# Joints between products in token halves, and retention in chunks of 128 tokens

## The chip, the cores and the metric

The kernel runs on one core of a Trainium2 chip. The metric is the device time of one execution in microseconds (us); before the change it was 2417.52, the median of three runs from 2414.93 to 2419.92. A core has TensorE (PE in the rows, its weight loads PEld), VectorE (DVE), ScalarE (ACT), GpSimd (POOL) and SyncE (SP), which issues the transfers here. Each engine works through its own instruction list in order and waits on semaphores for the others.

## The reference

Input `x` is 512 tokens by 1024 channels in float32. Two stacks of layers follow each other. The first has a mixer of four groups of heads (retention, gated delta, two gated linear ones), attention to a memory, and a feed-forward layer. The second has two layers, each with a mixer, a feed-forward part, norms before and after, and factors computed from a condition. What the change touches:

```python
def rms_norm(x, g):                                   # over the 1024 channels of a token
    y = x * lax.rsqrt(jnp.mean(x * x, axis=-1, keepdims=True) + EPS)
    return y * g

# second stack, layer i, twice (mixer, then feed-forward):
h = rms_norm(x, norm_pre) * (1.0 + sc) + sh
y = mixer(h)                                          # ends with @ w_out; the other ends with @ w_down
x = x + (1.0 + g) * rms_norm(y, norm_post)

# retention, one head, chunks of c tokens (the reference takes c = 64):
scores = (q @ k.T) * decay                            # decay = exp(lg * (i - j)) for i >= j, inside the chunk
o      = scores @ v + (q @ state) * exp(lg * (i + 1))
state  = state * exp(lg * c) + (k * exp(lg * (c - 1 - j))).T @ v
```

Every value of `c` gives the same `o`; one chunk of 512 needs no state.

## The kernel before

Activations lie with channels on the 128 partitions and tokens along a row: 1024 channels are 8 tiles (KT) of 128 x 512. A product's weights are streamed from memory by SyncE into a ring of six slots. A weight tile (up to 8 inner blocks of 128 x 128) is split by VectorE into a high and a low part (`split_until`, L344 and L346; ScalarE does some of the first), which needs one of three slots of `high`. Each inner step of an output tile is three matmuls in a rounded format, high x high, low x high and high x low (`passes`, L393 to L395), each on 512 token columns into one PSUM bank. `product` goes over the output tiles; with `lead=2` its first two output tiles advance together, inner step by inner step, as the input tiles become ready (`inputs_ready`).

**A joint** (`edge`, L451) is what lies between the last product of one part and the first of the next in the second stack: `ab_out` (16 inner steps) to `up_1`, `down_1` (22) to `sc_in`, `sc_out` (8) to `up_2`; and `down_2` (22) to the output. `plain_product` (L2671) computes the product before it: ScalarE takes each output tile out of PSUM twice, squared (L2699) and plain (L2701); GpSimd adds the squares (L419). Then, on 512 tokens at a time:

1. TensorE sums the squares over the channels, 128 equal columns per token block (L473, L476). ScalarE takes the root (L496), VectorE the reciprocal (L518), TensorE spreads it over the partitions (`spread_root`, L465).
2. Per tile j of 8: VectorE multiplies `y` by the factor and the gain (L530) and adds it to the residual `h` (L534); ScalarE squares the new `h` (L508); TensorE adds it up (L487).
3. Root, reciprocal and spread again. Per tile: VectorE scales `h` (L541), ScalarE adds the shift and rounds (L513), VectorE makes the low part (L547). The next product's led tiles take each tile as it comes.

`keep_busy` (L653, its matmul L656) issues n products of a constant that nobody reads: 11 ahead of step 2, one after each of its tiles, 8 after the second spread. In the last joint there is no step 3, and `store_output` (L3546) stores tile by tile behind L534.

**Retention** is a part of `mixers` (L1482), in the first stack. The order of TensorE's work there is written out by hand, one call after another (L1873 on). It is interleaved with a triangular inverse (`inverse_times`, L1679) in 32 x 32 pieces and followed by `join_first` (L1697), `join_second` (L1707, L1711). `ret_scores(i)` (L1650) computes for a pair of heads m and a key block j the scores of 128 keys with all later queries (512, 384, 256 or 128 columns), VectorE multiplies them by the decay (`ret_weight`, L2222, 16 operations of L2228), and `ret_values(i)` (L1663) adds the values product; eight such steps, through two pairs of score banks.

A float32 matmul (constants, sums, retention) stands in the trace as two pieces. The sections of the diff below name the functions again.

## Time and profile before

| what | value |
|---|---|
| median of three runs | 2417.52 us |
| the profiled execution's own time | 2420.88 us |
| its span, first to last instruction | 2419.1 us |
| mean granted TensorE clock | 0.973 |
| busy: PE, DVE, ACT, POOL | 2335.3, 1651.3, 663.9, 183.2 us |
| memory traffic | 253.94 MB, 105 GB/s |

The profile shows one execution. Busy time of an engine is the sum of its instructions' durations; matmuls overlap, so a busy PE can still be below its peak. "PEclk" is the clock that TensorE was granted as a share of full speed. A row in order of time has the start, the duration, engine, line, operation, output and inputs with their shape, the count of merged instructions, and in brackets how long the engine had been idle and who released it; "issue" means that nothing in the profile held it. Durations of neighbouring VectorE or ScalarE operations overlap a little, so the distance from start to start is the better price.

### The profile page before, as it was taken

Reading aid. Unit: us, or ns where it says so; the run is one execution under the profiler, and the core shown is the slowest. Engines: PE = TensorE matmul, PEld = TensorE weight load, DVE = VectorE, ACT = ScalarE, POOL = GpSimd, SP = SyncE. Lnnn points to the kernel's source line nnn. Section 1 sums busy time; section 2 is a strip of 40 time slices with the busy share of each in tenths; the row PEclk is TensorE's granted clock in tenths of the full one; section 3 lists DMA queues with packets and bytes.
Section 4 is the critical chain, followed back from the end, with each engine's and each line's share of the span. In section 5 each row is a group of like instructions: output and inputs, shape, how many; then the busy total and the mean of one; then the engine's idle time right before and its main releaser. Section 6 shows DMA issues by size and latency. Waiting matters only on the chain.

```text
span 2419.1 us, 35289 instructions
## 1 busy us (share of the span) xinstructions
PE 2335.3 (97%) x14624; PEld 1898.2 (78%) x14624; DVE 1651.3 (68%) x2569; ACT 663.9 (27%) x1200; POOL 183.2 (8%) x179
## 2 busy tenths in 40 slices
PE   8998879999999999999989999999999999999997
PEld 6886668878888888887756788888888888888886
DVE  6674366756888865559788777666667886666653
ACT  2321253022211201324768413222102113222200
POOL 0001222001000011003211010000010000000000
PEclk9999579999999999999999999999999999999998
DMA  4220003412222453322200361232562451322341
GB/s 183 79 79 2 21 3 122 158 52 88 96 96 96 135 204 130 107 81 92 88 1 2 138 219 62 98 100 97 197 214 104 182 186 63 102 96 96 127 141 64
DMA packets 71728, 253.94 MB, mean 105 GB/s; under 512 B 8560, under 2 KB 8848, under 8 KB 71056
## 3 DMA queue, kind: packets, MB, share of 16 engines
q1 hardware_dynamic: 71280, 251.14, 30.4%
q8 instruction: 116, 1.90, 0.3%
q10 hardware_dynamic: 288, 0.54, 0.1%
q14 instruction: 44, 0.36, 0.0%
HBM read 247.97 MB, written 2.10 MB: 103 GB/s over the span
## 4 chain that ended last, share of the span: by engine, by line
PE 47%; DVE 3%; issue 0%; ACT 0%; POOL 0%; DVEq 0%; POOLq 0%
PE psum L393 14%; PE psum L394 14%; PE psum L395 13%; PE psum L3362 1%; PE psum L487 1%; PE psum L3349 1%; PE psum L3384 1%; DVE scratch L3440 1%; DVE scratch L3416 1%; PE psum L656 0%; PE psum L3376 0%; PE psum L465 0%; DVE h L534 0%; DVE n L530 0%; PE psum L476 0%
## 5 line engine op out<-in xcount | busy, mean ns | idle before, releaser
L393 PE MATMUL psum<-rounded_n,rounded_high 128*128 128x512 f32 x1824 | 722.1, 396 | 8.0 <-DVE rounded_ring L346 4.6
L394 PE MATMUL psum<-rounded_n_low,rounded_high 128*128 128x512 f32 x1824 | 712.1, 390 | 0.0
L395 PE MATMUL psum<-rounded_n,rounded_ring 128*128 128x512 f32 x1824 | 712.0, 390 | 0.0
L346 DVE TENSOR_TENSOR rounded_ring<-ring,rounded_high 128x1024 fp32r<-128x1024 f32 (+1 forms) x360 | 448.4, 1246 | 43.5 <-ACT rounded_high L329 31.5
L393 PEld LDWEIGHTS psum<-rounded_n,rounded_high 128*128 128x128 f32 x1824 | 343.9, 189 | 86.6 <-issue 7.4
L394 PEld LDWEIGHTS psum<-rounded_n_low,rounded_high 128*128 128x128 f32 x1824 | 344.1, 189 | 74.2 <-issue 3.9
L395 PEld LDWEIGHTS psum<-rounded_n,rounded_ring 128*128 128x128 f32 x1824 | 343.7, 188 | 72.1
L344 DVE CAST rounded_high<-ring 128x1024 fp32r<-128x1024 f32 (+1 forms) x347 | 250.4, 722 | 188.3 <-PE psum L395 177.9
L393 PE MATMUL psum<-rounded_arena,rounded_high 128*128 128x512 f32 x720 | 280.2, 389 | 0.0
L395 PE MATMUL psum<-rounded_arena,rounded_ring 128*128 128x512 f32 x720 | 280.1, 389 | 0.0
L394 PE MATMUL psum<-rounded_arena,rounded_high 128*128 128x512 f32 x720 | 280.1, 389 | 0.0
L2617 DVE SCALAR_TENSOR_TENSOR scratch<-arena,vecs,scratch 128x512 f32<-128x512 f32 x88 | 65.9, 748 | 162.8 <-ACT scratch L2604 162.8
L393 PEld LDWEIGHTS psum<-rounded_arena,rounded_high 128*128 128x128 f32 x720 | 135.1, 188 | 28.3 <-issue 0.2
L395 PEld LDWEIGHTS psum<-rounded_arena,rounded_ring 128*128 128x128 f32 x720 | 135.1, 188 | 28.1
L394 PEld LDWEIGHTS psum<-rounded_arena,rounded_high 128*128 128x128 f32 x720 | 135.1, 188 | 27.9
L2598 ACT COPY arena<-psum 128x512 f32<-128x512 f32 x88 | 51.7, 587 | 351.2 <-PE psum L395 351.2
L2604 ACT ACTIVATE scratch<-arena,vecs 128x512 f32<-128x512 f32 x88 | 63.8, 725 | 188.4 <-DVE arena L2638 186.9
L2699 ACT ACTIVATE scratch<-psum 128x512 f32<-128x512 f32 x32 | 19.2, 600 | 317.4 <-PE psum L395 317.4
L419 POOL TENSOR_TENSOR sum_sq<-sum_sq,scratch 128x512 f32<-128x512 f32 x38 | 59.9, 1575 | 288.4 <-ACT scratch L2699 242.2
L416 POOL COPY sum_sq<-scratch 128x512 f32<-128x512 f32 x6 | 4.7, 786 | 955.4 <-ACT scratch L2699 820.0
L993 DVE CUSTOM_DVE_ANT_0 arena<-arena 128x1024 f32<-128x1024 f32 x48 | 61.9, 1333 | 13.4 <-DMA arena<-in_mod_w 13.4
L993 DVE CUSTOM_DVE_ANT_0 n_low<-n_low 128x1024 f32<-128x1024 f32 x48 | 56.7, 1221 | 19.9 <-DMA n_low<-in_mod_w 19.9
(507 smaller groups left out, 2798.3 us busy)
## 6 DMA issues: line engine op xcount, KB each, us to landing
ring<-in_w_up SPq DMA_DIRECT2D x132, 512.0 KB, 3.6
ring<-in_w_down SPq DMA_DIRECT2D x48, 512.0 KB, 3.5
n_low<-in_mod_w SPq DMA_DIRECT2D x48, 512.0 KB, 5.8
arena<-in_mod_w SPq DMA_DIRECT2D x48, 512.0 KB, 5.3
ring<-in_w_ab_in SPq DMA_DIRECT2D x37, 512.0 KB, 3.6
ring<-in_w_mix_in SPq DMA_DIRECT2D x31, 512.0 KB, 3.6
ring<-in_w_sc_in SPq DMA_DIRECT2D x24, 512.0 KB, 5.7
ring<-in_w_down SPq DMA_DIRECT2D x24, 384.0 KB, 3.0
```

Of the source, the lines that this page charges most:

```text
L344: nc.vector.tensor_copy(self.rounded(high), raw).then_inc(self.weights_rounded, 1)
L346: nc.vector.tensor_tensor(self.rounded(raw), raw, self.rounded(high), ALU.subtract).then_inc(self.weights_split, 1)
L393: self.nc.tensor.matmul(out, w_high, x_high, start=first, stop=False)
L394: self.nc.tensor.matmul(out, w_high, x_low, start=False, stop=False)
L395: return self.nc.tensor.matmul(out, w_low, x_high, start=False, stop=last)
L419: nc.gpsimd.tensor_tensor(total, total, sq, ALU.add).then_inc(added, 1)
L487: last = nc.tensor.matmul(k.psum[:, SUMS + c, P:2 * P], k.squares[:, j % 2, c * P:(c + 1) * P], ones, start=(j == 0), stop=(j == KT - 1))
L993: k.nc.vector.tensor_tensor_reduce(out=self.tiles[:, i % 3], in0=self.tiles[:, i % 3], in1=self.cond, scale=1.0, scalar=0.0, op0=ALU.mult, ...
L2598: nc.scalar.copy(x, k.psum[:, j % PRODUCT_BANKS, :]).then_inc(out, 1)
L2604: nc.scalar.activation(dst, x, ACT.Copy, scale=taps[:, col:col + 1]).then_inc(tapped, 1)
L2617: link(nc.vector.scalar_tensor_tensor(dst, src[:, 0:T], taps[:, col:col + 1], dst, ALU.mult, ALU.add))
L3349: last = nc.tensor.matmul(k.psum[:, 2 * (m % 2) + s, at * P:(at + nk) * P], k.z[rows, NQT + p, i * P:(i + 1) * P], k.z[rows, (KS, KW)[b] + ...
```

## The change

**Joints.** The last output tile of the product before a joint is computed as two halves of 256 tokens (`last_tile`), the second into another bank. The sums of half 0 are put between the matmuls of the second half (`meanwhile`): sums at inner step 2, the spread at 6, column sums of the new `h` at 13, 15, and so on. The sums have one column instead of 128. Updates, squares, scalings and low parts are done per half (h = 0, 1); five of eight residual additions per half go to GpSimd (`POOL_ADDS`). The next product's two led tiles run through all inner steps for half 0 and then for half 1 (`halves=2`), and half 1's updates, squares and column sums are placed beside half 0's steps (`beside`). How much of half 0 is placed ahead of the second half's eviction depends on the inner length: `early` is 8 for 22 steps, 4 for 16, 0 for 8; `late` (for 22) also shifts half 1 by two steps. The fillers are now 2, 2, 3 and 3 products. The output is stored in halves.

**Retention.** Scores are computed within chunks of 128 tokens only (16 products 128 x 128). The state at each chunk's start comes from `ret_grow` (12 products 64 x 64 of the keys, turned into token rows by 8 more transposes and weighted in `ret_tails`) and `ret_grown_states` (five short VectorE operations); `ret_values` adds state x query to scores x values. GpSimd scales the queries first (two operations). The 16 weightings are four of 512 columns.

On TensorE, at the joint after `ab_out`, a row of the program's order names the line, the operation, output and inputs, the columns and how often it is repeated. Before:

```order
L395 MATMUL psum<-rounded_arena,rounded_ring 128x512
L473 MATMUL psum<-consts,sum_sq 128x128 x4
L476 MATMUL psum<-consts,scratch 128x128 x4
L465 MATMUL psum<-consts,roots 128x128 x4
L656 MATMUL psum<-consts 128x128 x11
L487 MATMUL psum<-consts,scratch 128x128 x4
L656 MATMUL psum<-consts 128x128
```

At its end before:

```order
L487 MATMUL psum<-consts,scratch 128x128 x4
L465 MATMUL psum<-consts,roots 128x128 x4
L656 MATMUL psum<-consts 128x128 x8
L393 MATMUL psum<-rounded_n,rounded_high 128x512
L394 MATMUL psum<-rounded_n_low,rounded_high 128x512
L395 MATMUL psum<-rounded_n,rounded_ring 128x512
```

After, from the end of the last tile's second half (L421 to L423 are `passes`, L829 the filler, L542 a column sum of the new `h`, L526 and L527 the sums of half 1, L534 and L549 the two spreads):

```order
L423 MATMUL psum<-rounded_arena,rounded_ring 128x256
L542 MATMUL psum<-consts,scratch 128x1 x6
L526 MATMUL psum<-consts,sum_sq 128x1
L527 MATMUL psum<-consts,scratch 128x1
L526 MATMUL psum<-consts,sum_sq 128x1
L527 MATMUL psum<-consts,scratch 128x1
L829 MATMUL psum<-consts 128x128 x2
L542 MATMUL psum<-consts,scratch 128x1 x4
L829 MATMUL psum<-consts 128x128 x2
L542 MATMUL psum<-consts,scratch 128x1 x4
L534 MATMUL psum<-consts,roots 128x128 x2
L829 MATMUL psum<-consts 128x128 x3
```

The sums of half 0 have moved into the last tile, those of half 1 stand behind it, and the fillers are fewer and in other places.

On VectorE, the same joint before, from the last update of step 2 on (L530, L534) to the scalings and low parts of step 3 (L541, L547):

```order
L530 SCALAR_TENSOR_TENSOR n<-n,mod_cols,psum 128x512
L534 TENSOR_TENSOR h<-h,n 128x512
L518 RECIPROCAL roots<-roots 128x4
L541 SCALAR_TENSOR_TENSOR n_low<-h,mod_cols,psum 128x512 x2
L547 SCALAR_TENSOR_TENSOR rounded_n_low<-n_low,mod_cols,rounded_n 128x512
L541 SCALAR_TENSOR_TENSOR n_low<-h,mod_cols,psum 128x512
L547 SCALAR_TENSOR_TENSOR rounded_n_low<-n_low,mod_cols,rounded_n 128x512
```

After, from half 0's last update on; L664 and L668 are the update and the addition, L673 the scaling, L679 the low part, L349 and L351 the split of a weight tile:

```order
L668 TENSOR_TENSOR h<-h,n 128x256
L660 RECIPROCAL roots<-roots 128x2 x2
L349 CAST rounded_high<-ring 128x1024
L351 TENSOR_TENSOR rounded_ring<-ring,rounded_high 128x1024
L673 SCALAR_TENSOR_TENSOR n_low<-h,mod_cols,psum 128x256
L664 SCALAR_TENSOR_TENSOR n<-n,mod_cols,psum 128x256
L673 SCALAR_TENSOR_TENSOR n_low<-h,mod_cols,psum 128x256
L664 SCALAR_TENSOR_TENSOR n<-n,mod_cols,psum 128x256
L668 TENSOR_TENSOR h<-h,n 128x256
L679 SCALAR_TENSOR_TENSOR rounded_n_low<-n_low,mod_cols,rounded_n 128x256
```

A split and half 1's updates now stand between the scalings and the low parts of half 0.

On TensorE in the mixer, before, from the last steps of retention to the first joining product (L1660 scores, L1669 values, L1679 and L1697 the inverse):

```order
L1660 MATMUL psum<-z 128x384 x2
L1679 MATMUL psum<-ring 32x32 x64
L1669 MATMUL psum<-ring,n_low 64x512 x2
L1660 MATMUL psum<-z 128x256 x2
L1679 MATMUL psum<-high,ring 32x32 x64
L1669 MATMUL psum<-ring,n_low 64x384 x2
L1660 MATMUL psum<-z 128x128 x2
L1669 MATMUL psum<-ring,n_low 64x256 x2
L1697 MATMUL psum<-ring,n 32x32 x32
```

After (L1833 scores, L1868 and L1886 the inverse, L1780 transposes, L1843 the states' growth, L1859 values, L1855 state x query):

```order
L1780 MATMUL psum<-consts,z 128x128 x8
L1868 MATMUL psum<-ring 32x32 x64
L1833 MATMUL psum<-z 128x128 x8
L1868 MATMUL psum<-high,ring 32x32 x64
L1843 MATMUL psum<-n_low,n 64x64 x12
L1868 MATMUL psum<-ring 32x32 x64
L1868 MATMUL psum<-high,ring 32x32 x64
L1859 MATMUL psum<-ring,n_low 64x128 x2
L1855 MATMUL psum<-z,n 64x128 x2
```

The scores now stand in two groups ahead, and all the values products behind the inverse.

The diff, cut to its core:

```diff
+        for h in range(halves if lead > 1 else 0):
+            cols = tokens(h) if halves > 1 else slice(0, width)
+            for k in range(kt):
+                if inputs_ready is not None:
+                    pe.wait_ge(inputs_ready, kt * h + k + 1)
+                for j in range(lead):
+                    if h == 0 and k == 0:
+                        if banks_free is not None:
+                            pe.wait_ge(banks_free[0], banks_free[1] - PRODUCT_BANKS + j + 1)
+                        pe.wait_ge(self.weights_split, first + j + 1)
+                    x = [part[:, cols] for part in rhs(k)]
+                    last = self.passes(self.psum[:, j % PRODUCT_BANKS, cols], first + j, k, x, k == 0, k == kt - 1)
+                    if h == halves - 1 and k == kt - 1:
+                        last.then_inc(self.weights_used, 1)
+                if beside is not None:
+                    beside(kt * h + k)
...
+    def last_tile(self, pe, name, rhs, evacuated, first_half, meanwhile):
+
+        n_out, kt = PRODUCTS[name]
+        j, first = n_out - 1, self.first_tile[name] + (n_out - 1) * self.chunks(name)
+        for h in range(2):
+            pe.wait_ge(evacuated, j + h - PRODUCT_BANKS + 1)
+            out = self.psum[:, (j + h) % PRODUCT_BANKS, tokens(h)]
+            for kk in range(kt):
+                i = first + kk // SLOT_KT
+                if h == 0 and kk % SLOT_KT == 0:
+                    pe.wait_ge(self.weights_split, i + 1)
+                x = [part[:, tokens(h)] for part in rhs(kk)]
+                last = self.passes(out, i, kk % SLOT_KT, x, kk == 0, kk == kt - 1)
+                if h == 0 and kk == kt - 1:
+                    last.then_inc(first_half, 1)
+                if h == 1:
+                    if kk % SLOT_KT == SLOT_KT - 1 or kk == kt - 1:
+                        last.then_inc(self.weights_used, 1)
+                    meanwhile(kk)
...
+    kt = PRODUCTS[product][1]
+    early = 8 if kt > 16 else 4 if kt > 8 else 0
+    late = early == KT
+    lag = 2 if late else 0
...
+    def resums(pe, h, j):
+        pe.wait_ge(resquared, KT * h + j + 1)
+        for c in pieces(h):
+            last = nc.tensor.matmul(k.psum[:, RESUMS, c:c + 1], k.squares[:, j % 2, c * P:(c + 1) * P], one,
+                                    start=(j == 0 and c == 2 * h), stop=(j == KT - 1 and c == 2 * h + 1))
+        last.then_inc(counted, 1)
...
+        def meanwhile(kk):
+            if kk == 2:
+                sums(pe, 0)
+            if kk == 6:
+                spread_root(pe, 0)
+            if gain is not None and kk >= 13 and kk % 2 == 1:
+                resums(pe, 0, len(counts))
+                counts.append(kk)
+
+        k.last_tile(pe, product, rhs, out, halved, meanwhile)
         if gain is None:
+            sums(pe, 1)
+            spread_root(pe, 1)
             return
         pe.wait_ge(out, KT - 2)
-        keep_busy(k, pe, 11)
-        for j in range(KT):
-            pe.wait_ge(resquared, j + 1)
-            for c in range(TT):
-                last = nc.tensor.matmul(k.psum[:, SUMS + c, P:2 * P], k.squares[:, j % 2, c * P:(c + 1) * P], ones,
-                                        start=(j == 0), stop=(j == KT - 1))
-            last.then_inc(counted, 1)
-            if j < KT - 1:
-                keep_busy(k, pe, 1)
-        spread_root(pe, 1)
-        keep_busy(k, pe, 8)
...
+        for j in range(len(counts), early):
+            resums(pe, 0, j)
+        if not late:
+            sums(pe, 1)
+        for j in range(early, KT):
+            if j % 2 == 0:
+                keep_busy(k, pe, 2)
+            resums(pe, 0, j)
+        if late:
+            keep_busy(k, pe, 3)
+            spread_again(pe, 0)
+            sums(pe, 1)
+        else:
+            spread_root(pe, 1)
+            keep_busy(k, pe, 3)
+            spread_again(pe, 0)
+        keep_busy(k, pe, 3)
+        pe.wait_ge(out, KT + 1)
...
+            if lag + 2 <= x < KT:
+                resums(pe, 1, x - lag - 2)
+            if x == KT - 1:
+                for j in range(KT - lag - 2, KT):
+                    resums(pe, 1, j)
+                spread_again(pe, 1)
...
+            if j == early:
+                second_half()
+            square(0, j)
         act.wait_ge(counted, KT)
-        root(act, 1)
+        root(act, RESUMS, 1, 0, rerooted)
+        if late:
+            second_half()
...
+            raise_high(0, j)
+            if j >= lag + 1:
+                square(1, j - lag - 1)
+        for j in range(KT - lag - 1, KT):
+            square(1, j)
+        act.wait_ge(counted, 2 * KT)
+        root(act, RESUMS, 1, 1, rerooted)
+        for j in range(KT):
+            raise_high(1, j)
...
+        def update(h, j):
+            at = tokens(h)
+            nc.vector.scalar_tensor_tensor(y[:, j, at], y[:, j, at], first_gain[:, j:j + 1],
+                                           k.psum[:, SPREAD[h], at], ALU.mult, ALU.mult).then_inc(stepped, 1)
+            if j not in POOL_ADDS:
+                dve.wait_ge(stepped, KT * h + j + 1)
+                nc.vector.tensor_tensor(k.h[:, j, at], k.h[:, j, at], y[:, j, at], ALU.add).then_inc(renewed, 1)
...
+        following = k.first_tile[then]
+        k.split_until(dve, following + 1)
+        if not late:
+            invert(0, 1, rooted, inverted)
+        invert(1, 0, rerooted, reinverted)
+        k.split_until(dve, following + 2)
+        dve.wait_ge(respread, 1)
+        for j in range(KT + lag):
+            if j < KT:
+                scale(0, j)
+            if late and j == 0:
+                invert(0, 1, rooted, inverted)
+            if j == lag:
+                dve.wait_ge(spread, 2)
+                dve.wait_ge(out, KT + 1)
+            if j >= lag:
+                update(1, j - lag)
+            if 1 <= j <= KT:
+                low_part(0, j - 1)
+        if lag == 0:
+            low_part(0, KT - 1)
+        k.split_until(dve, following + 3)
+        invert(1, 1, rerooted, reinverted)
+        dve.wait_ge(respread, 2)
...
+            for c in range(TT - 1):
+                for h in range(HEADS):
+                    at, own = HD * (2 * c + h // 2), slice(h * HD, (h + 1) * HD)
+                    last = nc.tensor.matmul(k.psum[head_rows(h), G0, at:at + HD], k.ret_keys[:, c, own],
+                                            k.v_tok[:, 0, c, own], start=True, stop=True)
+            last.then_inc(ret_grown, 1)
+
+        def ret_values(m):
...
+            for c in range(TT):
+                cols = slice(c * P, (c + 1) * P)
+                if c >= 1:
+                    for s in range(2):
+                        rows = head_rows(s)
+                        nc.tensor.matmul(k.psum[rows, G0 + 2 + m, cols], k.ret_state[rows, c - 1, m, :],
+                                         z[rows, RQ + m, cols], start=True, stop=False)
+                for s in range(2):
+                    h = 2 * m + s
+                    last = nc.tensor.matmul(k.psum[head_rows(s), G0 + 2 + m, cols],
+                                            k.v_tok[:, 0, c, h * HD:(h + 1) * HD], k.ret_w[h][:, cols],
+                                            start=(c == 0), stop=True)
...
         inverse_times(2)
         ret_scores(0)
+        inverse_update(2)
+        turn(KEYS_TURN)
+        inverse_times(3)
         ret_scores(1)
-        inverse_update(2)
+        inverse_update(3)
+        ret_grow()
+        inverse_times(4)
+        inverse_update(4)
         ret_values(0)
-        ret_scores(2)
-        inverse_times(3)
+        join_first()
         ret_values(1)
-        ret_scores(3)
-        inverse_update(3)
-        ret_values(2)
-        ret_scores(4)
-        ret_values(3)
-        ret_scores(5)
-        inverse_times(4)
-        ret_values(4)
-        ret_scores(6)
-        inverse_update(4)
-        ret_values(5)
-        ret_scores(7)
-        ret_values(6)
-        join_first()
-        ret_values(7)
         join_second()
...
+        def ret_weight(m):
+            dve.wait_ge(ret_scored, m + 1)
             for s in range(2):
-                nc.vector.tensor_tensor(k.ret_w[2 * (i % 2) + s][:, 0:T - j * P],
-                                        k.psum[:, RET_BANK[i % 2] + s, 0:T - j * P],
-                                        k.const(f"decay{2 * m + s}")[:, 0:T - j * P], ALU.mult
+                h = 2 * m + s
+                mask = k.const("ret_mask")[:, h * P:(h + 1) * P].unsqueeze(1).broadcast_to([P, TT, P])
+                nc.vector.tensor_tensor(blocks(k.ret_w[h]), blocks(k.psum[:, RET_BANK[m] + s, :]), mask, ALU.mult
```

## Rows read from the trace of the kernel before

**Rows 1.** The page's part 1: busy time and share of the span.

```profile
PE 2335.3 (97%) x14624; PEld 1898.2 (78%) x14624; DVE 1651.3 (68%) x2569; ACT 663.9 (27%) x1200; POOL 183.2 (8%) x179
```

**Rows 2.** The joint after `ab_out` in time order; then a led step.

```profile
1446.29 1.05 PE L473 MATMUL psum<-consts,sum_sq 128*128 128x128 f32 x8
...
1446.59 0.69 DVE L344 CAST rounded_high<-ring 128x1024 fp32r<-128x1024 f32 x1 [3.02 <-PE psum L395]
...
1447.31 1.23 DVE L346 TENSOR_TENSOR rounded_ring<-ring,rounded_high 128x1024 fp32r<-128x1024 f32 x1
1448.34 0.26 ACT L496 ACTIVATE roots<-psum,consts 128x4 f32<-128x4 f32 x1 [0.78 <-PE psum L476]
1448.64 0.18 DVE L518 RECIPROCAL roots<-roots 128x4 f32<-128x4 f32 x1
...
1450.07 0.75 DVE L530 SCALAR_TENSOR_TENSOR n<-n,mod_cols,psum 128x512 f32<-128x512 f32 x1 [1.25 <-PE psum L465]
1450.85 0.69 DVE L534 TENSOR_TENSOR h<-h,n 128x512 f32<-128x512 f32 x1
1451.46 0.74 DVE L530 SCALAR_TENSOR_TENSOR n<-n,mod_cols,psum 128x512 f32<-128x512 f32 x1
...
1467.21 0.50 PE L393 MATMUL psum<-rounded_n,rounded_high 128*128 128x512 f32 x1 [0.60 <-DVE rounded_n_low L547]
...
1470.78 0.39 PE L393 MATMUL psum<-rounded_n,rounded_high 128*128 128x512 f32 x1
...
1471.46 0.39 PE L393 MATMUL psum<-rounded_n,rounded_high 128*128 128x512 f32 x1
```

**Rows 3.** A stretch of that joint: engines' busy time, PEclk, DMA share, GB/s.

```profile
1450.00:1460.00 10.00, 9.99 (x80) 9.04 (x79) 9.70 (x15) 3.90 (x7) 0.00 (x0) 1.00 0.01 2
```

**Rows 4.** 256-column matmuls of the memory attention, in order of time.

```profile
424.76 0.28 PE L393 MATMUL psum<-rounded_upper,rounded_high 128*128 128x256 f32 x1
424.88 0.28 PE L394 MATMUL psum<-rounded_upper,rounded_high 128*128 128x256 f32 x1
```

**Rows 5.** 256-column operations of VectorE, ScalarE, GpSimd: ns shortest/median/longest.

```profile
L689 DVE SCALAR_TENSOR_TENSOR rounded_upper<-upper,vecs,rounded_upper x8: 476/478/479, 390.9 to 406.8; 128x256 fp32r<-128x256 f32 x8
...
L676 ACT ACTIVATE scratch<-upper x8: 402/418/418, 379.3 to 385.9; 128x256 f32<-128x256 f32 x8
...
L2141 POOL TENSOR_TENSOR scratch<-upper x21: 612/613/994, 224.3 to 345.0; 128x256 f32<-128x256 f32 x21
```

**Rows 6.** Narrow float32 pieces, the matmuls behind them, and that stretch's clock.

```profile
67.74 3.63 PE L1069 MATMUL psum<-consts,upper 128*128 128x2 f32 x32
...
73.24 0.63 PE L394 MATMUL psum<-rounded_n_low,rounded_high 128*128 128x512 f32 x1
...
71.00:80.00 9.00, 9.00 (x33) 6.56 (x33) 3.70 (x7) 3.71 (x7) 0.00 (x0) 0.81 0.00 0
```

**Rows 7.** GpSimd's add of squares beside a split's second half, in order of time.

```profile
1436.29 1.56 POOL L419 TENSOR_TENSOR sum_sq<-sum_sq,scratch 128x512 f32<-128x512 f32 x1 [8.81 <-ACT scratch L2699]
...
1436.74 2.19 DVE L346 TENSOR_TENSOR rounded_ring<-ring,rounded_high 128x1024 fp32r<-128x1024 f32 x1
```

**Rows 8.** The last joint, in order of time.

```profile
2401.67 1.05 PE L473 MATMUL psum<-consts,sum_sq 128*128 128x128 f32 x8
...
2415.98 0.69 DVE L534 TENSOR_TENSOR h<-h,n 128x512 f32<-128x512 f32 x1
```

**Rows 9.** The retention stretch in order of time; then L2228, and L1679's idle time.

```profile
227.83 1.15 PE L1679 MATMUL psum<-high,ring 32*32 32x32 f32 x112 [0.34 <-issue]
...
231.46 1.22 PE L1679 MATMUL psum<-ring 32*32 32x32 f32 x121 [0.59 <-issue]
...
253.58 0.26 PE L1707 MATMUL psum<-high,ring 32*32 32x32 f32 x1
...
L2228 DVE TENSOR_TENSOR ring<-psum,consts x16: 252/467/692, 226.6 to 251.2; 128x512 f32<-128x512 f32 x4, 128x384 f32<-128x384 f32 x4, 128x256 f32<-128x256 f32 x4, 128x128 f32<-128x128 f32 x4
...
  issue: 11.2, 17
```

324 lines of the change are left out of this document (196 added, 128 removed).

## The prediction

> **What bounds the kernel now.** I read the busy line first, then the joint after `ab_out` in order of time, then the granted clock of that stretch, then the last joint, and last the retention stretch. TensorE is busy for 97% of the span [rows 1]: where it works on wide products the pace is its own, so the change can only gain where TensorE waits, and it loses wherever it adds TensorE work or makes TensorE wait longer.
>
> The joint after `ab_out` is such a place [rows 2]. The first of the column sums starts at 1446.29, when the last product matmul has been issued; the first matmul of the next product starts at 1467.21. Between them lie 20.9 us without a product. The reader should see what paces them. The row sums, root, reciprocal and spread take 1446.29 to 1450.07 (3.8 us). Eight tiles follow, one per 1.39 us (1450.07 to 1451.46), each an L530 and an L534 on VectorE, so VectorE sets that pace. After eight of them, at 1461.2, the last square and sum, root, reciprocal, spread, two scalings, the shift and the low part take the other 6.0 us. After that the first two tiles of the next product go step by step, 0.68 us a step for six matmuls (1470.78 to 1471.46), so a matmul every 0.227, while VectorE needs a scaling and a low part, about 2 x 0.67 (L530's 0.75 less an overlap of 0.08), per step of 1.36 with two tiles' worth of matmuls: 48 x 0.227 = 10.9 us. The granted clock was 1.00, its higher level (2.4 GHz), from 1450 to 1460, as before and behind [rows 3]: TensorE was kept at work there by filler products (L656): eleven, one after each tile, and eight at the end.
>
> I count each joint from the start of the previous product's last tile to the end of the two led tiles. Before, with 16 inner steps (`ab_out`): 48 x 0.227 = 10.9, plus 20.9, plus 10.9 = 42.7. With 22 (`down_1`) it is 46.8, with 8 (`sc_out`) 37.2, since the dead part is the same there by the same instructions.
>
> **The joint after the change, `ab_out`.** Prices of 256-column operations: a matmul every 0.12 us [rows 4]; on VectorE 0.48 busy, 0.40 from one to the next (the 512-wide ones overlap by 0.08 in rows 2, and I take that off); on ScalarE 0.42 [rows 5]; a one-column float matmul has no row, and two-column ones take 3.63 us for 32 pieces, 0.113 each [rows 6]. I take 0.115; nothing shows less than that for a 128-row piece, and two pieces a matmul.
> (a) The last tile in halves: 96 x 0.12 = 11.5, plus four sums (8 pieces, 0.9), a spread (0.45) and two of the new column sums (8 pieces, 0.9) = 13.8. Before 10.9.
> (b) From there to the first next product matmul. The first half of the tile ends at 5.8; with sums, root, reciprocal and spread (in TensorE's order only after 21 more matmuls) VectorE can start on half 0 at about 9.8. Its eight updates at 0.40 and three adds at 0.35 take 4.3; the adds of five tiles go to GpSimd. But ScalarE squares tiles 0 to 3 of half 0, then turns to the second half of the last tile, which is ready at 13.8 (two evictions, 0.9, and a root that waits for four more sums), and only then squares tiles 4 to 7 at 0.42 each, each followed by its column sum of 0.46: about 19.0. Root 0.26, reciprocal 0.18, spread 0.45 and six filler matmuls bring 20.8. VectorE meanwhile splits a weight tile, 1.9 (L344 and L346 of rows 2, 0.69 + 1.23), to 21.6, since that stands ahead of the scaling in its order; scale, update, scale, update, add and the first low part (0.40, 0.40, 0.40, 0.40, 0.35, 0.48) end at 24.0. So (b) is 10.2. Before 20.9.
> (c) Half 0 of the two led tiles. TensorE needs 6 x 0.12 = 0.72 a step and 0.46 for half 1's column sum. VectorE has a scaling of half 0, an update of half 1 and a low part of half 0 per step, 3 x 0.40 = 1.20, with an add at tiles 1, 4 and 7. Seven steps of 1.20, two adds and the last step's six matmuls with its sum: 10.3.
> (d) The turn to half 1: four column sums 1.8, root 0.26, reciprocal 0.18, spread 0.6, scale 0.48, shift 0.50, low part 0.48, hand-overs 0.3 = 4.6 (root, reciprocal: rows 2, L496 and L518). Nothing covers it: no tile can run until half 1's factors exist.
> (e) Half 1: seven steps of 0.80 and the last of 0.72 = 6.3.
> Sum 13.8 + 10.2 + 10.3 + 4.6 + 6.3 = 45.2 against 42.7: +2.5. What (b) saves, 10.7, goes back as 2.9 in (a) and 10.3 in (c) to (e). For `down_1` (early = 8) the same sum gives 48.7 against 46.8, +1.9; for `sc_out` (early = 0, eight inner steps, so little to hide in) 40.2 against 37.2, +3.0. The three together +7.5. GpSimd's adds next to VectorE are a term of their own. A split's second half (L346), 1.23 in rows 2, took 2.19 while GpSimd's L419 ran [rows 7]. Ten adds of 0.61 [rows 5] a joint, of which most run beside updates that read PSUM: I take 0.4 a joint, bounds 0 and 6. Joints: +8.7.
> The Trainium skill ("SBUF — State Buffer", section on SBUF's two separate sides) says that VectorE with two SBUF inputs and a GpSimd operation that reads SBUF exclude each other for a whole instruction. The trace agrees, 2.19 against 1.23. By that rule alone the adds would cost up to their full length, which is the upper bound's reason, not its number.
>
> **The clock.** After the product matmuls of 60 to 67 the 32 two-column pieces at 67.74 kept TensorE formally busy for 3.6 us; behind them the granted clock of 71 to 80 was 0.81, and a 512-column L394 took 0.63 instead of 0.39 [rows 6], about 0.213 for each 256-column half plus the fixed part: the lower level (1.2 GHz) for a part of it: 0.81 over 9 us are 3.4 us at half speed. The change makes (b) of one-column sums with only 2 to 3 filler matmuls where 11 and 8 stood, and (d) nearly empty. I expect the lower level in each joint. At it a step of (c) costs 6 x 0.213 + 0.46 = 1.74 in place of 1.33, eight steps 3.3; in (e) 1.28 in place of 0.80, eight steps 3.8. Bounds 0 and 7 a joint. In rows 6 it rose again once the wide matmuls were back, so I take (c) alone, 3.3. Three joints: +10.
>
> **The last joint.** From the start of the sums (2401.67) to the last L534's end (2415.98 + 0.69) were 15.0 us, the store's end at 2419.1 is 2.4 behind [rows 8]. With a last tile of 66 matmuls (15.0 us at 0.227) the last update ends 30.0 after that tile's start. In halves: the tile 132 x 0.12 = 15.8, sums and spread of half 0 within it 1.4, half 1's eviction, sums, root, reciprocal and spread 4.5, eight updates and the adds 4.3 = 26.0; half 0's updates are hidden in the tile. The stores are twice as many, but all except the last lie earlier. -4.0, bounds -5 and -2.
>
> **Retention.** VectorE's 16 weightings (7.5 us together, median 0.467 [rows 9]) become four of 0.69, and GpSimd, otherwise idle there, scales the queries; 12 small products, 8 transposes, a 128 x 1024 product of about 1.2 and five short operations come in. By this chain of VectorE and TensorE alone the stage's end mark, the start of L1707 at 253.58, would come 8 to 11 us sooner. But the rows of L1679 show another limit: 17 waits on "issue", 11.2 us in all; two of them, at 227.83 and 231.46, are 128 matmuls and 3.63 us apart [rows 9]. That is the pace at which instructions arrive, whatever the engines do, and the change has 32 more products, 64 pieces, up to that mark. A block edge lies two blocks before 227.83, at 220.5. From there to the mark are some 1000 pieces by TensorE's order, 7.8 blocks or 28.5 us, of the 33.1 measured; the other 4.6 are the chain's. With 1064 pieces, 8.3 blocks, and no chain left it is 220.5 + 8.3 x 3.65 = 250.8, -2.8. I take -2.5; bounds -11 (the chain alone) and +2 (one stall more). The Trainium skill ("Runtime: NRT & Kernel Launch", section on instruction fetch) calls this refill mostly hidden; here the trace differs, with 11.2 us. By that rule it would be the chain's -8 to -11.
> The tables in the constants shrink and are loaded ahead of use: nothing, hidden by the first product.
>
> **Sum.** +8.7 + 10 - 4.0 - 2.5 = +12. On the profiled execution's own 2420.9 us (span 2419.1 and 1.8 around it) that is 2433; this execution lay 3.4 above the median of 2417.5, so the median after is 2417.5 + 12 = 2429.5, I say 2429.
>
> **Rivals.** *The clock holds.* The fillers left and the led tiles are enough; the joints keep +8.7: +2, time 2419.5. For it: the clock was 1.00 through all of a joint whose TensorE work was 128-wide pieces [rows 3]. Against it: the fall after rows 6's narrow pieces, and (d) is emptier still.
> *Faster: VectorE's half-width operations cost half.* The place is (b), (c) and (e). If a 256-column operation took 0.33 (half of 0.67) and an add 0.30, (c)'s step would be 1.0, (b) 1.0 shorter, (e) limited by TensorE at 0.72: 1.0 + 1.6 + 0.6 + 0.3 in (d) = 3.5 a joint, 10.5 in all, and TensorE at 1.18 of work a step would never stand idle in (c), so the clock would hold. +2 - 10.5 = -8.5: 2409. It decides from about 0.36 per operation. Against it are eight rows of 0.48 (L689), which write the same type; but they read no PSUM.
> *The clock stays low, or GpSimd locks VectorE.* The lower level through (c), (d) and (e) costs 7 a joint, or the adds half their 6: +22, 2440.
> *Retention freed of the waits for instructions:* the chain alone decides, -9.5 instead of -2.5, from about 2.9 us per 128 pieces; 2422 with all else as forecast. Against it are the 11.2 us of rows 9; 0.1 of the chance, held in the forecast's.
> *The change doesn't do what it says in the mixer:* retention is bound by fetch entirely, +2 instead of -2.5; it lies in the range.
>
> **Chances.** Forecast 0.47 (its own range 2423 to 2437), clock holds 0.20, faster 0.21, low throughout 0.12. A measurement here tells about 0.2%, 4.8 us, from no change. Faster by more than that: the faster rival and a little of the second, 0.25. Within: 0.17, mostly the clock holding, and the low edge of the forecast. Slower: 0.58. The range leaves out about half of the faster case and of the lowest clock: 2408 to 2440.
>
> **What would show it.** Right: in each joint the first product matmul about 10 us after the last tile, steps of 1.2 to 1.7 us in half 0, a hole of 4 to 5 us between the halves, a granted clock under 1 there, three joints of 41 to 52 us by my count, the last update 4 us sooner, the product that answers to L1707 starting between 249 and 252. Wrong: steps under 1.1; the clock at 1.00 across the joints; squares of tiles 4 to 7 ahead of the second half's root; retention's mark before 245, or the clock of the 32-wide stretches behind it moved by more than a microsecond or two, which I have left at nothing.

## The result and the profile after

The changed kernel takes 2446.07 us in the median of four runs (2442.96 to 2449.8); the kernel before took 2416.7 in the median of four (2414.93 to 2419.92). The ratio is 1.0118 with a 95% interval of 1.0106 to 1.013: about 29 us slower. The forecast was 2429 with a range up to 2440: the direction was right, the size not, and the range missed the time.

The profiled execution's span is 2448.0 us, 28.9 more than before. The page's first parts after:

```profile
span 2448.0 us, 36138 instructions
...
PE 2358.5 (96%) x14932; PEld 1941.6 (79%) x14932; DVE 1657.6 (68%) x2642; ACT 675.3 (28%) x1263; POOL 215.2 (9%) x221
...
PEclk9999579999999999999999998999998998999999
```

TensorE's busy time is 23.2 us more, VectorE's only 6.3 more [rows 1], so TensorE is the place to look. The mean granted clock fell from 0.973 to 0.958. Where it went can be read by comparing the start of the same weight split (L346 before, L351 after; both have 360 of them) in the two traces: the 28.9 us are +4.2 behind retention, +13.3 at the joint after `ab_out`, +5.5 after `down_1`, +10.2 after `sc_out`, and -4.3 at the last joint.

Each joint counted as in the prediction, from the last tile's first matmul to the end of the two led tiles, in us:

| joint | before | forecast without the clock | after | with wide sums (e3) |
|---|---|---|---|---|
| `ab_out` | 42.9 | 45.2 | 55.7 | 46.4 |
| `down_1` | 46.9 | 48.7 | 52.3 | 49.2 |
| `sc_out` | 37.4 | 40.2 | 47.5 | 40.8 |
| sum over before | | +7.5 (+8.7 with GpSimd's share) | +28.4 | +9.2 |

The joint after `ab_out` of the changed kernel, TensorE in order of time (L542: column sum, L829: filler, L421: product, L549: second spread):

```profile
1453.03 1.68 PE L542 MATMUL psum<-consts,scratch 128*128 128x1 f32 x12
...
1456.81 1.71 PE L542 MATMUL psum<-consts,scratch 128*128 128x1 f32 x8
1458.37 1.20 PE L829 MATMUL psum<-consts 128*128 128x128 f32 x4
1459.37 1.71 PE L542 MATMUL psum<-consts,scratch 128*128 128x1 f32 x8
...
1466.92 0.36 PE L421 MATMUL psum<-rounded_n,rounded_high 128*128 128x256 f32 x1 [1.42 <-issue]
...
1474.95 0.85 PE L542 MATMUL psum<-consts,scratch 128*128 128x1 f32 x4
...
1484.45 1.22 PE L549 MATMUL psum<-consts,roots 128*128 128x128 f32 x4 [0.55 <-DVE roots L660]
1487.31 0.58 PE L421 MATMUL psum<-rounded_n,rounded_high 128*128 128x256 f32 x1 [1.63 <-DVE rounded_n_low L679]
```

Before, eight pieces took 1.05 to 1.16 us and the gap between product matmuls was 21.1 us [rows 2]. Here the product's last matmul is issued at 1452.91 and the next product's first at 1466.92, a gap of 14.0 instead of the 10.2 forecast. The reader should look at the durations: eight one-column pieces take 1.71 and the next instruction starts 1.56 behind them, 0.195 a piece; four filler pieces take 1.20. Neither VectorE nor ScalarE is named as a releaser in the gap, and TensorE sits idle only for its last 1.42 us: TensorE itself is the slow one. Stretches of the same joint, with the columns of rows 3:

```profile
1446.00:1452.00 6.00, 6.00 (x54) 6.00 (x53) 2.57 (x7) 1.35 (x5) 1.13 (x2) 1.00 0.18 50
1452.00:1458.00 6.00, 5.88 (x42) 5.79 (x40) 3.58 (x7) 2.48 (x8) 2.44 (x4) 0.76 0.37 129
1458.00:1464.00 6.00, 6.00 (x29) 6.00 (x29) 2.00 (x3) 0.85 (x3) 0.00 (x0) 0.50 0.00 0
1468.00:1480.00 12.00, 11.88 (x57) 11.57 (x57) 8.10 (x20) 3.84 (x10) 2.96 (x4) 0.53 0.01 1
1480.00:1486.00 6.00, 5.12 (x23) 4.74 (x22) 1.67 (x3) 1.10 (x3) 0.00 (x0) 0.50 0.00 0
```

The granted clock falls in the second of these stretches (by the trace's clock records at 1455.1), is at 0.50 from then on, and again, after a short recovery, from 1468.7 to 1492.6, through most of the led tiles and the turn. Before it was 1.00 through the whole joint; rows 3 show 1450 to 1460. TensorE was "busy" for 5.88 of 6.00 us in the stretch of the fall and for 6.00 of 6.00 in the next one, as in rows 6.

Retention after, TensorE in order of time (L1868 the inverse, L1859 scores x values, L1855 state x query, L1896 the joining product that was L1707 [rows 9]); then two stretches of it, a stretch before, and L1868's idle time on "issue":

```profile
247.69 0.85 PE L1868 MATMUL psum<-high,ring 32*32 32x32 f32 x43 [1.45 <-issue]
248.47 0.70 PE L1859 MATMUL psum<-ring,n_low 128*64 128x128 f32 x4
249.09 0.69 PE L1855 MATMUL psum<-z,n 64*64 64x128 f32 x4
...
258.42 0.69 PE L1859 MATMUL psum<-ring,n_low 128*64 128x128 f32 x4
259.05 0.26 PE L1896 MATMUL psum<-high,ring 32*32 32x32 f32 x1
```

```profile
244.00:259.00 15.00, 12.77 (x291) 7.85 (x290) 4.18 (x10) 1.17 (x2) 5.31 (x8) 0.59 0.01 3
248.50:259.00 10.50, 10.50 (x121) 5.86 (x120) 2.17 (x4) 1.17 (x2) 5.31 (x8) 0.50 0.01 3
```

```profile
244.00:252.30 8.30, 6.31 (x266) 3.69 (x254) 4.90 (x11) 0.00 (x0) 1.59 (x3) 1.00 0.02 4
```

```profile
  issue: 16.7, 14
```

The mark comes at 259.05 instead of 253.58, 5.5 us late instead of 2.5 early. The inverse ends at 248.5 and nothing waits for instructions behind it; what stands there are 28 products, 14 groups of four pieces, 0.62 us each from start to start at a granted clock of 0.50: 8.7 us, and L1886 between them (1.85 us). Before, the clock was 1.00 from 244 to 252.3, nearly up to the mark.

The last joint after (columns as in rows 8):

```profile
2437.39 0.38 PE L526 MATMUL psum<-consts,sum_sq 128*128 128x1 f32 x2 [0.47 <-ACT scratch L2895]
...
2439.74 0.87 DVE L664 SCALAR_TENSOR_TENSOR n<-n,mod_cols,psum 128x256 f32<-128x256 f32 x2 [0.80 <-PE psum L534]
...
2444.67 0.95 DVE L668 TENSOR_TENSOR h<-h,n 128x256 f32<-128x256 f32 x1
```

The last addition ends at 2445.6, and the span 2.4 us later, as before [rows 8].

### The profile page after: what moved, and what is told of

The parts are those of the page before. It is cut to its first block, busy times and chain, and to the rows that moved or that the text cites. A ratio compares the mean times of both kernels' runs of the same rounds, so it can differ in the third digit from the quotient of the medians.

```text
span 2448.0 us, 36138 instructions
## 1 busy us (share of the span) xinstructions
PE 2358.5 (96%) x14932; PEld 1941.6 (79%) x14932; DVE 1657.6 (68%) x2642; ACT 675.3 (28%) x1263; POOL 215.2 (9%) x221
## 4 chain that ended last, share of the span: by engine, by line
PE 46%; DVE 3%; issue 1%; ACT 0%; POOL 0%; ACTq 0%; POOLq 0%
PE psum L421 14%; PE psum L423 13%; PE psum L422 13%; PE psum L3574 1%; PE psum L3561 1%; PE psum L3596 1%; PE psum L542 1%; DVE scratch L3652 1%; DVE scratch L3628 1%; PE psum L829 0%; PE psum L3588 0%; DVE n L664 0%; DVE rounded_n_low L679 0%; PE psum L534 0%; PE psum L549 0%
## 5 line engine op out<-in xcount | busy, mean ns | idle before, releaser
L421 PE MATMUL psum<-rounded_n,rounded_high 128*128 128x512 f32 (+1 forms) x1872 | 740.1, 395 | 16.7 <-DVE rounded_n_low L679 7.8
L422 PE MATMUL psum<-rounded_n_low,rounded_high 128*128 128x512 f32 (+1 forms) x1872 | 727.4, 389 | 0.0
L423 PE MATMUL psum<-rounded_n,rounded_ring 128*128 128x512 f32 (+1 forms) x1872 | 727.1, 388 | 0.0
L351 DVE TENSOR_TENSOR rounded_ring<-ring,rounded_high 128x1024 fp32r<-128x1024 f32 (+1 forms) x360 | 448.0, 1245 | 43.1 <-ACT rounded_high L334 31.1
L421 PEld LDWEIGHTS psum<-rounded_n,rounded_high 128*128 128x128 f32 x1872 | 360.1, 192 | 94.6 <-issue 10.5
L422 PEld LDWEIGHTS psum<-rounded_n_low,rounded_high 128*128 128x128 f32 x1872 | 360.3, 192 | 72.4 <-issue 3.9
L423 PEld LDWEIGHTS psum<-rounded_n,rounded_ring 128*128 128x128 f32 x1872 | 359.9, 192 | 70.4
L349 DVE CAST rounded_high<-ring 128x1024 fp32r<-128x1024 f32 (+1 forms) x347 | 250.3, 721 | 172.7 <-PE psum L423 162.3
L421 PE MATMUL psum<-rounded_arena,rounded_high 128*128 128x512 f32 (+1 forms) x788 | 293.4, 372 | 0.0
L422 PE MATMUL psum<-rounded_arena,rounded_high 128*128 128x512 f32 (+1 forms) x788 | 292.3, 371 | 0.0
L423 PE MATMUL psum<-rounded_arena,rounded_ring 128*128 128x512 f32 (+1 forms) x788 | 292.3, 371 | 0.0
L421 PEld LDWEIGHTS psum<-rounded_arena,rounded_high 128*128 128x128 f32 x788 | 148.5, 188 | 25.7 <-issue 0.2
L422 PEld LDWEIGHTS psum<-rounded_arena,rounded_high 128*128 128x128 f32 x788 | 148.5, 188 | 25.6
L423 PEld LDWEIGHTS psum<-rounded_arena,rounded_ring 128*128 128x128 f32 x788 | 148.5, 188 | 25.2
L2906 ACT ACTIVATE scratch<-psum 128x512 f32<-128x512 f32 x28 | 16.8, 600 | 275.7 <-PE psum L423 275.7
```

What stands on the lines that cost most here:

```text
L349: nc.vector.tensor_copy(self.rounded(high), raw).then_inc(self.weights_rounded, 1)
L351: nc.vector.tensor_tensor(self.rounded(raw), raw, self.rounded(high), ALU.subtract).then_inc(self.weights_split, 1)
L421: self.nc.tensor.matmul(out, w_high, x_high, start=first, stop=False)
L422: self.nc.tensor.matmul(out, w_high, x_low, start=False, stop=False)
L423: return self.nc.tensor.matmul(out, w_low, x_high, start=False, stop=last)
```

## The experiments

Medians are given with the ratio to the kernel before, which ran on the same chip beside each group; its median differs by up to 6 us between groups (2416.7 to 2422.9), so times of different groups are compared by their ratios. In the profiled executions the stretch ahead of the joints differs too, though its code is the same: the last tile of `ab_out` starts at 1429.7 us in e2 and at 1439.1 in e4, and 8 of these 9 us come about between 192 and 353 us, in the mixer. So joints are compared by their own lengths in the traces, counted as in the table above.

**e1 and e2: the parts alone.** Retention's parts of the diff without the joints', and the reverse.

> Only the retention part of the change; the joints are as before. By the two traces the split of the first weight tile behind retention comes 4.2 us later than before, and joints make up the rest of the 28.9 us. Theory A (the stage loses by its own added small products, all of which now stand behind the inverse, and by waits for instructions): 4 us slower, 2421. Rival B (retention alone gains, and what is lost there comes from the joints' code, since it shifts where instructions are fetched): 2 to 3 us faster, 2414.

Measured 2423.87, ratio 1.0021 (1.0009 to 1.0034), which is 5 us slower, mark at 259.15: A. The mark alone would be weaker evidence: in the eleven traces with unchanged retention it lies between 253.5 and 259.3. They fall into two kinds. In seven of them (before, e2, e5, e6, e7, e9, e16) the clock was low for one spell of 3.4 us near 215, and the mark is at 253.5 to 256.0, mean 254.7; in four (e3, e4, e13, e14) that spell lasted 6.8 us, and the mark is at 257.4 to 259.3. The changed kernel and e1 are of the first kind, so against their like they are 4.4 us late, with 3.1 to 5.6 as the span.

> Only the joints of the change; retention is as before. Theory A (the two parts add up): 2416.7 + 13.6 + 5.5 + 10.1 - 4.3 = 2441.6. Rival B (the parts work on each other): outside 2438 to 2445.

Measured 2438.29, ratio 1.0076 (1.0048 to 1.0105). The gaps in its trace are those of the changed kernel within 0.1 us (13.94, 6.17, 17.23), so in the joints the parts don't work on each other. The total lies 3 us below A's sum by the median and 6 by the ratio, whose interval still holds A's sum.

**e3: the width of the sums.** One edit in the joints, the number of matmuls unchanged:

```diff
-    one = k.const("ones")[:, 0:1]
+    ones = k.const("ones")
-            last = nc.tensor.matmul(k.psum[:, RESUMS, c:c + 1], k.squares[:, j % 2, c * P:(c + 1) * P], one,
+            last = nc.tensor.matmul(k.psum[:, RESUMS, c * P:(c + 1) * P], k.squares[:, j % 2, c * P:(c + 1) * P], ones,
```

(`sums` likewise; ScalarE's root reads one column of each block.)

> Joints of the change with the sums over 128 equal columns, as before the change, in place of one column; same number of matmuls, same order, same fillers, retention as before. A piece took 0.115 us with one column and 0.112 with 128 at the higher clock, so the work itself is the same. Theory A (one-column sums let the clock fall, and at the lower level they take 0.195 a piece): the gap after ab_out shrinks from 14.0 to about 10.5, after sc_out from 17.3 to 12.5, half 0 and half 1 of the led tiles run at the higher clock; total 16 to 20 us less than the joints alone, 2422 to 2426. Rival B (the order of work on VectorE and ScalarE sets the gaps, the clock only follows): gaps within 1 us of 14.0 and 17.3, 2438 or more. Rival C (the sparse fillers are the cause, not the width of the sums): granted clock still half behind each last tile, less than 5 us gained.

Measured 2424.05, ratio 1.0017 (1.0002 to 1.0032). The same place in its trace, in order of time (L538: column sum, L826: filler), and stretches:

```profile
1447.57 1.89 PE L538 MATMUL psum<-consts,scratch 128*128 128x128 f32 x12
...
1452.00 0.61 PE L826 MATMUL psum<-consts 128*128 128x128 f32 x4
1452.45 1.06 PE L538 MATMUL psum<-consts,scratch 128*128 128x128 f32 x8
```

```profile
1447.00:1453.00 6.00, 5.67 (x48) 5.29 (x47) 3.16 (x6) 3.07 (x9) 2.00 (x3) 1.00 0.26 91
1453.00:1458.00 5.00, 2.74 (x25) 2.55 (x23) 4.09 (x9) 1.60 (x4) 0.73 (x1) 1.00 0.00 0
1458.00:1470.00 12.00, 10.94 (x71) 10.28 (x72) 10.05 (x24) 5.01 (x12) 3.52 (x4) 0.86 0.00 0
```

Eight pieces are back at 1.06 to 1.16 us and the clock at 1.00, although TensorE is less busy than with the change (2.74 of 5.00 us from 1453 to 1458). The gaps are 10.94, 6.38 and 12.02; the forecast's (b) after `ab_out` was 10.2. 14 us of the change's loss hang on this one edit by the ratios, with both runs on one chip, and 19.1 by the lengths of the three joints. A holds in the main, with a little less than its 16 to 20 us in time, and B and C are out; but half 0 of the led tiles did not run at the higher clock throughout: 0.86 shows that 3.4 us at the lower level are left, after `ab_out` and again after `sc_out`. The first begins at 1459.9, 2 us behind the stretch in which TensorE was busy for 2.74 of 5.00 us.

**e4 and e13: fillers.** e4 adds fillers to e3, e13 the same fillers to one-column sums:

```diff
-            if j % 2 == 0:
-                keep_busy(k, pe, 2)
+            keep_busy(k, pe, 2)
...
-        keep_busy(k, pe, 3)
+        keep_busy(k, pe, 8)
```

> As the run with wide sums, with more fillers too: two before each column sum of half 0 behind the last tile, 5 or 4 ahead of the second spread, 8 behind it, and 4 and 8 in the turn to half 1. Theory A (with the clock held everywhere a joint costs what the forecast's sum without the clock term says, +8.7 for the three): 2416.7 + 8 - 4.3 = 2421, granted clock 1.00 in all joints. Rival B (joints cost more than that sum at full clock too): 2426 or more at a clock of 1.00. Rival C (the fillers themselves stand in the way): slower than the run without them.

Measured 2426.08, ratio 1.0035 (1.0022 to 1.0049), no lower clock left in any of the three joints; gaps 11.8, 6.5, 14.0. Nearer to C than to A: 2 to 4 us above e3 with intervals that overlap, and 2.8 us more in the lengths of the three joints. What the last of the lower clock cost is not more than what the fillers take. The measured time at a clock of 1.00 also meets B as it was put; the joints are 12.1 us longer than before, fillers included, where the forecast's sum said 8.7.

> Joints of the change with its own one-column sums and the larger fillers of the run with wide sums and fillers (two before each column sum, 4 or 5 and 8 around the second spread, 4 and 8 in the turn); retention as before. Theory A (the width of the sums is the cause; fillers of one in three pieces are not enough): the clock falls in the dead part after ab_out and sc_out as with the change, 2435 or more. Rival B (the fillers that the change removed are the cause): clock 1.00 there and 2424 to 2428, as with wide sums.

Measured 2438.41, ratio 1.0071 (1.0053 to 1.0089). Stretches behind the last tile after `ab_out`:

```profile
1451.60:1457.00 5.40, 5.28 (x35) 5.20 (x34) 2.70 (x6) 2.24 (x7) 1.53 (x3) 0.71 0.31 100
1457.00:1464.00 7.00, 7.00 (x35) 7.00 (x34) 2.00 (x3) 0.68 (x2) 0.00 (x0) 0.50 0.00 0
```

The gaps are 15.7, 8.0 and 13.9. After `ab_out` A holds: more fillers between one-column sums do not hold the clock, though the led tiles' low stretch went (none in the 30 us behind the gap, against 23.9 with the change), and the gap grew. After `down_1` it fell for three short stretches. After `sc_out` A was wrong: the clock stayed at 1.00 there. The median is that of e2, 2438, and the ratios (1.0071 and 1.0076) don't tell the two apart. But the three joints are 145.7 us long here and 155.5 in e2: 9.8 us less, all of it in the led tiles, while the gaps are the same in sum; this execution was 8.7 us later than e2's before the first joint. So the fillers give back about half of what the wide sums do (19.1).

**e7: the width alone, in the kernel before.**

```diff
-    ones = k.const("ones")
+    ones = k.const("ones")[:, 0:1]
-            nc.tensor.matmul(k.psum[:, SUMS + c, 0:P], k.sum_sq[:, c * P:(c + 1) * P], ones, start=True, stop=False)
+            nc.tensor.matmul(k.psum[:, SUMS + c, 0:1], k.sum_sq[:, c * P:(c + 1) * P], ones, start=True, stop=False)
...
```

> The kernel before with one thing changed: the sums of the three joints and of the last have one column instead of 128; fillers, order and counts as before. Theory A (the width of the sums alone lowers the clock): in each of three joints the column sums of a tile take 8 x 0.195 + 2 x 0.25 = 2.1 instead of 1.39 us a tile, and part of the led tiles runs at half speed: 5 to 12 us a joint, 2432 to 2453. Rival B (the fillers hold the clock whatever the sums are): 2417, clock 1.00 in the joints.

Measured 2435.57, ratio 1.0055 (1.0035 to 1.0075). TensorE in the joint after `ab_out`, ahead of the fall and behind it, and stretches:

```profile
1450.56 1.05 PE L487 MATMUL psum<-consts,scratch 128*128 128x1 f32 x8
1451.48 0.47 PE L656 MATMUL psum<-consts 128*128 128x128 f32 x2
...
1457.76 1.71 PE L487 MATMUL psum<-consts,scratch 128*128 128x1 f32 x8
1459.33 0.77 PE L656 MATMUL psum<-consts 128*128 128x128 f32 x2
```

```profile
1450.00:1460.00 10.00, 9.99 (x57) 9.42 (x56) 6.60 (x10) 3.66 (x6) 0.00 (x0) 0.66 0.01 2
1460.00:1467.00 7.00, 6.44 (x32) 6.35 (x32) 2.77 (x5) 1.64 (x3) 0.00 (x0) 0.51 0.00 0
1467.00:1480.00 13.00, 13.00 (x61) 10.78 (x60) 9.16 (x16) 6.14 (x9) 0.00 (x0) 1.00 0.10 31
```

A tile's eight sum pieces take 1.05 us first and 1.71 then, its filler 0.47 and 0.77, and the gap grows from 21.1 to 25.4, 26.2 and 27.6 in the three joints, 15.8 us in their lengths. Nothing else was changed, so the one-column sums lower the clock even with the 22 and 2 filler pieces of before: A in kind and B out. The size is just under A's low end (13 us slower in time against 15); the led tiles ran at 1.00 here.

**e6: GpSimd's adds.** `POOL_ADDS = ()` in e3.

> As the run with wide sums, but all residual additions on VectorE, none on GpSimd. Theory A (the adds on GpSimd save VectorE 0.35 us each, of which the three joints have some ten each, and hold up VectorE little): 3 joints x 3 to 10 adds x 0.3 = 3 to 9 us slower than with them, 2427 to 2433. Rival B (GpSimd and VectorE exclude each other, so the adds cost VectorE their 0.6 us anyway): no change or up to 5 us faster, 2419 to 2424.

Measured 2432.0, ratio 1.0042 (1.0027 to 1.0057). The additions' durations (ns shortest/median/longest) on VectorE and GpSimd with the change, then on VectorE in e6:

```profile
L668 DVE TENSOR_TENSOR h<-h,n x24: 424/670/978, 1450.5 to 2444.7; 128x256 f32<-128x256 f32 x24
```

```profile
L653 POOL TENSOR_TENSOR h<-h,n x40: 719/733/916, 1450.1 to 2444.6; 128x256 f32<-128x256 f32 x40
```

```profile
L665 DVE TENSOR_TENSOR h<-h,n x64: 424/424/428, 1442.0 to 2426.1; 128x256 f32<-128x256 f32 x64
```

The median of 0.67 hides three cases. With the change, nine of VectorE's 24 additions have no GpSimd addition beside them and take 0.42 to 0.43. The other 15 start while one is running, and each of them ends 0.28 us after that one: 0.66 to 0.67 where GpSimd's started 0.35 us earlier, 0.95 to 0.98 where it started 0.05 us earlier. In the last joint, in order of time:

```profile
2432.13 0.74 POOL L653 TENSOR_TENSOR h<-h,n 128x256 f32<-128x256 f32 x1 [9.55 <-DVE n L664]
2432.47 0.67 DVE L668 TENSOR_TENSOR h<-h,n 128x256 f32<-128x256 f32 x1
```

So VectorE's addition waits for GpSimd's to end, and three of them a joint cost it 1.3 us. But an addition moved away saves its whole 0.35 to 0.42, and three of eight stay. Without GpSimd the gaps grow to 11.4, 6.4 and 12.8, and the three joints are 7.1 us longer than in e3; 13.6 us instead of 6.8 at the lower clock are a part of that. By the medians over their own kernels before, e6 lies 3 us above e3, by the ratios 6, with intervals that overlap a little: A at its low end, and not B.

**e8: where retention's products stand.** Retention as in e1, with `ret_values` split into scores x values and state x query (`ret_carried`):

```diff
         ret_grow()
+        ret_values(0)
         inverse_times(4)
+        ret_values(1)
         inverse_update(4)
-        ret_values(0)
+        ret_carried(0)
         join_first()
-        ret_values(1)
+        ret_carried(1)
         join_second()
```

> Retention of the change alone, with the 16 products scores x values issued ahead of and between the inverse's last steps, and only the 12 products state x query behind it; joints as before. Theory A (the 28 products behind the inverse, 0.62 us per pair-group of four pieces at the lower clock, are what costs 4.7 us): 32 of 56 pieces less there, 5 us off that place, so the joining products start 3 to 5 us sooner than with the change and the total is 2418 to 2420. Rival B (instructions arrive too slowly there, whatever the order): no gain, 2423.

Measured 2417.99, ratio 0.998 (0.9962 to 0.9997): faster than before, and 10 us below e1 by the ratios, with intervals that allow 5 to 15. TensorE in order of time (L1685 scores x values, L1695 state x query, L1731 the mark), and the stretch up to it:

```profile
241.66 1.92 PE L1685 MATMUL psum<-ring,n_low 128*64 128x128 f32 x16
...
244.86 1.09 PE L1685 MATMUL psum<-ring,n_low 128*64 128x128 f32 x16
...
248.33 0.87 PE L1695 MATMUL psum<-z,n 64*64 64x128 f32 x12
...
252.59 0.21 PE L1731 MATMUL psum<-high,ring 32*32 32x32 f32 x1
```

```profile
244.00:252.60 8.60, 6.33 (x343) 5.44 (x330) 4.19 (x10) 1.17 (x2) 2.37 (x4) 1.00 0.02 6
```

The mark is at 252.59, 6.6 us sooner than in e1. 32 of the 56 pieces stand in front, at 0.07 to 0.12 us each; the 24 behind the inverse run at a granted clock of 1.00, 0.87 us for twelve. At that clock they cost 1.7 us, where at e1's 0.62 a group of four they would cost 3.7. So two things changed at once, the number of pieces behind the inverse and the clock at which they run, and no run separates them. A, and more. The traces of the two kernels are 6.6 us apart at the mark, 6.3 at the start of `ab_out`'s last tile and 6.1 in the execution's time, so nothing further was gained behind the mark; the 10 by the ratios is the same effect within its interval. The other traces with early values bear it out: e12 and e15, of the kind of e1, have the mark at 252.3 and 252.0, and e10, e11 and e17, of the other kind, at 254.6 to 255.6.

**e5: the last joint alone.**

> Of the change only the last joint in halves (down_2 to the output); the other three joints and retention as before. Forecast and both traces: the last update 4.0 to 4.3 us sooner, stores hidden. Theory A: 4 us faster than before, 2413 to 2414. Rival B (the halved stores or the longer last tile take it back): within 1 us of before.

Measured 2418.08, ratio 0.9981 (0.9967 to 0.9995), 4.6 us faster: A.

**e9, e14 and e16: another form of the joints.** Last tile in halves, half 0's update beside its second half, wide sums, but one second norm for all 512 tokens and the led tiles at full width as before:

```diff
-        k.product(pe, name, k.normed, T, out, inputs_ready=before.signals["done"], lead=2, halves=2, beside=...)
+        k.product(pe, name, k.normed, T, out, inputs_ready=before.signals["done"], lead=2)
...
+        for j in range(KT):
+            resums(pe, 1, j)
+        for c in range(TT):
+            last = nc.tensor.matmul(k.psum[:, 7, c * P:(c + 1) * P], k.roots[:, 1, c:c + 1].broadcast_to([P, P]), ...
```

> Joints in a third form, retention as before: last tile in halves with half 0's norm beside its second half, 128-column sums and fillers as in the run with wide sums, updates per half with GpSimd's adds; but the second norm is taken once for all 512 tokens, and the next product's two led tiles run at full width as before the change. By the sum of the forecast, counted from the last tile's start: after ab_out 13.8 (tile in halves) + half 1's eviction, sums, root, spread 2.9 + eight updates at 0.53 with GpSimd's adds 4.3 + last add, square, sum, root, spread 2.5 + two scalings, shift, low part 2.9 = 26.4, plus 10.9 led = 37.3, against 42.7 before. Theory A (what the change loses is in (c) to (e), the led tiles in halves at VectorE's pace, and the saving in the dead part is real): three joints 4 to 6 us each faster than before, last joint 4: 2401 to 2408. Rival B (halving itself costs what it saves, also in the dead part): 2415 or more.

Measured 2415.32, ratio 0.9973 (0.996 to 0.9987). Faster than before by 6.5 us, but 4.6 of them are the last joint's, and the other three gave nothing instead of 12 to 18: by the trace they are 42.8, 46.2 and 39.3 us long, 1.1 more in sum than before. In the joints that is B; the time, 2410 on the scale of 2417, lies between the two. The clock was 1.00 in all three. The gaps were 18.7, 16.4 and 21.3, where the estimate had 12.6 after `ab_out`. VectorE after `ab_out` (L881 reciprocals of half 1, L885 its updates, L917 the second reciprocal):

```profile
1451.33 0.16 DVE L881 RECIPROCAL roots<-roots 128x2 f32<-128x2 f32 x1
1453.96 0.87 DVE L885 SCALAR_TENSOR_TENSOR n<-n,mod_cols,psum 128x256 f32<-128x256 f32 x2 [2.47 <-PE psum L771]
...
1461.81 0.18 DVE L917 RECIPROCAL roots<-roots 128x4 f32<-128x4 f32 x1
```

Half 1's updates wait 2.5 us for their spread, which stood behind half 0's column sums on TensorE. Moving it ahead (e14):

> The third form of the joints with half 1's root taken, inverted and spread ahead of the weight split and of half 0's last column sums, and one filler instead of two per column sum. Theory A (half 1's updates waited for that spread): they start 1.5 us earlier after ab_out, 2408 to 2411 on the scale of 2417. Rival B (ScalarE's sixteen squares and their column sums are the pace): no change from the third form, 2411 to 2413.

Measured 2420.09, ratio 0.9991 (0.9978 to 1.0005). Gaps 16.8, 21.5, 18.2: shorter after `ab_out` and `sc_out`, longer after `down_1`, where 6.8 us at the lower clock appeared; the three joints are 1.3 us longer than before in sum. Neither A nor B as put. With the old order after `down_1` only (e16):

> The third form of the joints with half 1's spread moved ahead after ab_out and sc_out only, as in the first third form after down_1; last joint in halves; retention as before. Theory A (the gaps add as measured: 16.8, 16.4, 18.2 against 21.1 three times, less 2.9 for each last tile in halves and 0.5 for its end): 1.4 + 1.6 + 0 = about 3 to 5 us from the three joints and 4.5 from the last, 2410 on the scale of 2417. Rival B (the wait moves elsewhere again): 2413 or more.

Measured 2414.94, ratio 0.9975 (0.9964 to 0.9987): not told apart from e9. By its trace the three joints are 41.0, 46.2 and 36.2 us long, 3.8 less in sum than before, and the time is 2411 on the scale of 2417: A, though B's 2413 is inside the interval. The estimate of 12 to 18 us for this form has failed. The shorter gaps give so little because the last tile in halves takes it back: from its first matmul to its last it is 2.5 us longer after `ab_out`, 4.1 after `down_1` and 1.8 after `sc_out`, 8.3 of the 12.0 by which e16's gaps are shorter.

**e10, e11, e12, e15, e17: together.** e10 is the whole change with wide sums and early values, e11 the last joint and early values, e12 e9 with early values, e15 and e17 the same on e14 and e16.

> The whole change with two edits: 128-column sums in the joints and scores x values ahead of the inverse's last steps. Theory A (the effects add): joints with wide sums +6, early values -4.9: 1 us above before, 2418. Rival B (the two parts disturb each other): more than 3 us off that.

Measured 2423.24, ratio 1.0012 (0.9997 to 1.0027): 3 us above before by the ratio, 4 by the medians, and the interval holds A's 1.

> The two gains alone: the last joint in halves and retention with early values, the other joints as before. Sum of the two runs: -4.6 and -4.9, 2407. Rival B (they do not add): -5 only.

Measured 2414.09, ratio 0.9973 (0.9958 to 0.9987): -6.5, between A and B, and the interval holds both.

> The third form of the joints, the last joint in halves, and retention with early values. If theory A of the third form holds: 4.9 us below that run, 2396 to 2403.

Measured 2412.7, ratio 0.997 (0.9956 to 0.9984): -7. The condition was not met, and the range was missed.

> The same with the last joint in halves, as there, and the early values of retention. Between 2 and 5 us below the run before it.

Measured 2415.29, ratio 0.9978 (0.9966 to 0.9989), 3 to 5 us below e14: as expected.

> The same with retention's early values: 3 to 5 us below the run before it, 2405 to 2407 on the scale of 2417, the lowest of all.

Measured 2408.3, ratio 0.9966 (0.9954 to 0.9977): 8 us faster than before by the ratio, 10 by the medians, the lowest of all, but not told apart from e12 or e16, and just above the 2405 to 2407 expected (2408 to 2409 on that scale). e10 shows that two edits take back 26 of the change's 29 us by the ratios.

## Why the prediction was wrong, point by point

- **(a) to (e) without the clock: right.** +7.5, with GpSimd's share +8.7, against +9.2 in e3; each joint within 1.2 us. The turn (d) was forecast at 4.6 and measured at 4.9 in two joints of e3, 6.2 in the third.
- **The clock: right in kind, half the size.** "Three joints: +10" measured 28.4 - 9.2 = 19.2. The step that failed is "so I take (c) alone, 3.3", out of bounds of 0 to 7 a joint. The change's joints less e3's, part by part, in us:

  | joint | (b) | (c) | (d) | (e) | sum |
  |---|---|---|---|---|---|
  | `ab_out` | 3.1 | 3.1 | 1.3 | 1.9 | 9.3 |
  | `down_1` | -0.1 | 1.5 | -0.3 | 2.0 | 3.1 |
  | `sc_out` | 5.3 | -0.1 | 0 | 1.6 | 6.8 |
  | all three | 8.2 | 4.5 | 1.0 | 5.5 | 19.2 |

  So (c), forecast at 10 in all, measured 4.5. Two parts that had no term measured most of the rest: 8.2 in (b), where at the lower level the column sums and fillers become the pace (one-column pieces take 0.195 instead of 0.115), and 5.5 in (e), which was set aside because the clock would rise again once the wide matmuls were back; it stayed low for 4.6 to 5.5 us into each half 1. Inside (c) a step at the lower level took 2.13 (from 1472.81 to 1474.95), not 1.74, since the forecast kept its column sum at the higher clock's 0.46. The reason named, "one-column sums with only 2 to 3 filler matmuls", mixed two causes. e3 and e7 show that the width of the sums does it by itself; e13 that more fillers make up for it only in part, and e4 that beside wide sums more of them bring nothing.
- **The last joint: right.** -4.0 forecast, -4.3 in the trace, -4.6 alone (e5).
- **Retention: wrong side.** "I take -2.5" became +5.5 at the mark, +4.4 against traces of its kind, and +4 to +5 in the time (e1). The first step that failed is the one that made the arrival of instructions the only limit: "8.3 blocks, and no chain left". Waits on "issue" did grow, from 11.2 us to 16.7, but they end at 247.7; the 28 products behind the inverse had no price beyond their arrival and take 8.7 us there. The second is the clock of this stage, for which the sum had no term at all (it names only that of the stretches behind the mark, "which I have left at nothing"): it was 0.50 through all of these products. An estimate from the prices of the higher clock (twelve pieces in 0.87 us in e8; 1.13 for L1697's 64 pieces before, against L1886's 1.85) puts the 10.5 us behind the inverse at 5.2, so about 5.3 us of the loss are the clock's. The upper bound of +2 had no term for either. e8 shows that the order does it: with 16 of the products in front, the clock is 1.00 there and the mark is 6.6 us sooner. Why that order keeps the clock up was not tested.
- **GpSimd's adds: small, but more than taken.** Three additions a joint that wait for GpSimd's cost VectorE 1.3 us, not 0.4, within the bounds of 0 and 6. Of the rule on the shared port in the Trainium skill ("SBUF — State Buffer", the section on SBUF's two separate sides), the trace bears out the whole: each of the 15 additions that start beside GpSimd's ends 0.28 us after it, as if it had to wait for all of it.
- **The rivals.** "The clock stays low" was nearest, at 2440. Its 7 a joint, 21 in all, come near the 19.2, but by luck: in (c) to (e) the clock cost 11.0, and the other 8.2 lay in (b), for which it had no term either. With the 7 by which retention was off it would have been 2447. Together the two misses close the account: 12 + 9 for the clock + 7 for retention are 28 us, and 29 were measured. "VectorE's half-width operations cost half" was wrong: they take 0.47 and 0.48 us, also where they read PSUM (L664), as L689 had shown [rows 5].

## What to carry to other kernels

A matmul that writes one column where 128 equal ones were written costs the same per piece at the higher clock, and here it cost the clock: before narrowing such products, look at the granted clock of the stretch, and measure it again behind the edit. A lower clock is to be priced in every stretch that it may cover, the small products and fillers included, which then become the bound themselves. And products that are moved behind the last step of a serial chain have a price of their own, even where the engine seems to wait for something else all the time. One trace of each kernel is not enough to size an effect of 4 us here: unchanged code reached the same mark 5.8 us apart.

## What was not expected of the hardware

- TensorE can be busy for nearly the whole of a stretch, by the records, while its granted clock falls: 5.88 of 6.00 us from 1452 with the change, 9.99 of 10.00 in e7. With 128-column sums it was 1.00 in a stretch with 2.74 of 5.00 (e3), and only then fell, for 3.4 us.
- One-column float32 pieces take 0.115 us at the higher and 0.195 at the lower clock, 1.7 times as long.
- An addition of 128 x 256 on VectorE takes 0.42 us alone. Started while GpSimd's addition (0.73) runs, it ends 0.28 us after that one, 0.66 to 0.98 us long, in 15 of 15 cases.
